# Blocks 0 to 2 of h behind four stages turned by VectorE and SBUF-to-SBUF moves instead of TensorE

## What is computed

```
h = x + 0.5 * swiglu(rmsnorm(h, ffn1_norm), ffn1_w_in, ffn1_w_out)
u = rmsnorm(h, mix_norm) @ w_in_mix
h = h + concat(y_pool, y_gla) @ w_out_mix
h = h + 0.5 * swiglu(rmsnorm(h, ffn2_norm), ffn2_w_in, ffn2_w_out)
x = rmsnorm(h, final_norm)
h = mixer_a(x, w_in_a, w_o_a);  x = layer_norm(ALPHA * x + h)
x = x + (p @ w_ple) * sigmoid(x @ w_ple_gate)
k, v = x @ w_kv_b;  h = mixer_b(x, w_in_b, w_o_b, k, v);  ...
```

## Time and profile before

| | us |
|---|---|
| median of 3 runs | 2770.53 (2770.22 to 2772.04) |
| the profiled execution's own time | 2770.9 |
| its span, first to last instruction | 2769.1 |
| PE busy | 2731.3 |
| DVE busy | 1527.7 |
| ACT busy | 1290.0 |
| POOL busy | 63.6 |

### The profile page before, as it was taken

The page is one execution under the profiler, slowest core; times in us unless marked ns, Lnnn a source line. Parts: engine busy times, 40 slices in busy tenths (PEclk is TensorE's granted clock), DMA queues, the critical chain, the costliest instruction groups (busy, mean ns, idle before and its releaser), DMA issues.

```text
span 2769.1 us, 34994 instructions
## 1 busy us (share of the span) xinstructions
PE 2731.3 (99%) x12382; PEld 2244.7 (81%) x12382; DVE 1527.7 (55%) x1831; ACT 1290.0 (47%) x1691; POOL 63.6 (2%) x72
## 2 busy tenths in 40 slices
PE   7999999999999999999999999999999999999998
PEld 6888888888888788888888888887888888777877
DVE  4555555555644455555555555658555566555566
ACT  4443444344544454443444344544544454554463
POOL 1000000000000000000000000030000000120000
PEclk9999999999999999999999999999999999999999
DMA  7766567666644455765566666654465565445653
GB/s 225 223 215 199 181 196 226 192 195 195 199 148 158 149 194 160 223 218 193 182 201 224 195 195 190 200 174 153 144 202 176 168 196 190 152 140 192 188 176 130
DMA packets 404697, 516.09 MB, mean 186 GB/s; under 512 B 45750, under 2 KB 257920, under 8 KB 403792
## 3 DMA queue, kind: packets, MB, share of 16 engines
q1 hardware_dynamic: 402560, 505.84, 58.3%
q0 software_dynamic: 1824, 8.37, 0.9%
q10 hardware_dynamic: 176, 0.07, 0.0%
HBM read 502.06 MB, written 2.10 MB: 182 GB/s over the span
## 4 chain that ended last, share of the span: by engine, by line
PE 95%; DVE 2%; ACT 1%; POOL 1%; DMA 1%; SPq 1%; issue 0%; ACTq 0%; DVEq 0%; POOLq 0%
PE bank L1284 30%; PE bank L1286 30%; PE bank L1285 30%; PE bank L1242 1%; DMA h<-in_x_dram 1%; DVE wlo L1550 1%; POOL rope_b L858 1%; PE bank L1005 0%; PE bank L806 0%; ACT whi L1353 0%; PE bank L790 0%; PE bank L1022 0%; PE bank L1031 0%; SPq L1149 0%; DVE isc L915 0%
## 5 line engine op out<-in xcount | busy, mean ns | idle before, releaser
L1550 DVE TENSOR_TENSOR wlo<-raw,whi 128x1024 fp32r<-128x1024 f32 (+2 forms) x976 | 1149.4, 1186 | 1047.8 <-ACT whi L1353 1041.5
L1353 ACT CAST whi<-raw 128x1024 fp32r<-128x1024 f32 (+2 forms) x976 | 984.2, 1016 | 1206.8 <-PE bank L1286 1201.4
L1284 PE MATMUL bank<-whi,p_hi 128*128 128x512 f32 x2016 | 797.4, 396 | 4.0 <-DVE wlo L1550 4.0
L1286 PE MATMUL bank<-whi,p_lo 128*128 128x512 f32 x2016 | 786.9, 390 | 0.0
L1285 PE MATMUL bank<-wlo,p_hi 128*128 128x512 f32 x2016 | 786.6, 390 | 0.0
L1284 PE MATMUL bank<-whi,q_hi 128*128 128x512 f32 x1696 | 665.5, 392 | 1.6 <-DVE wlo L1550 1.6
L1286 PE MATMUL bank<-whi,q_lo 128*128 128x512 f32 x1696 | 660.5, 389 | 0.0
L1285 PE MATMUL bank<-wlo,q_hi 128*128 128x512 f32 x1696 | 660.0, 389 | 0.0
L1284 PEld LDWEIGHTS bank<-whi,p_hi 128*128 128x128 f32 x2016 | 379.7, 188 | 88.9 <-issue 10.0
L1285 PEld LDWEIGHTS bank<-wlo,p_hi 128*128 128x128 f32 x2016 | 379.7, 188 | 80.2 <-issue 3.1
L1286 PEld LDWEIGHTS bank<-whi,p_lo 128*128 128x128 f32 x2016 | 379.5, 188 | 80.3
(11 more groups left out here) (265 smaller groups left out, 1032.2 us busy)
## 6 DMA issues: line engine op xcount, KB each, us to landing
raw<-in_ffn_w_in_dram SPq DMA_DIRECT2D x704, 256.0 KB, 4.4
raw<-in_ffn_w_out_dram SPq DMA_DIRECT2D x320, 256.0 KB, 3.5
raw<-in_w_in_a_dram SPq DMA_DIRECT2D x192, 256.0 KB, 3.0
raw<-in_w_in_mix_dram SPq DMA_DIRECT2D x128, 256.0 KB, 3.1
raw<-in_w_ple_gate_dram SPq DMA_DIRECT2D x128, 256.0 KB, 3.6
raw<-in_w_in_b_dram SPq DMA_DIRECT2D x128, 256.0 KB, 3.1
raw<-in_w_out_mix_dram SPq DMA_DIRECT2D x64, 256.0 KB, 3.1
raw<-in_w_o_a_dram SPq DMA_DIRECT2D x64, 256.0 KB, 3.3
```

The costliest lines, as they stand in the source:

```text
L1284: pe.matmul(o, xht, wh, start=(kt == t_first), stop=False)
L1286: ins = pe.matmul(o, xlt, wh, start=False, stop=(kt == t_last))
L1353: act.copy(whi[:, c % SPLIT, 0:n, 0:w], raw[:, c, 0:n, 0:w]).then_inc(hi_done, 1)
L1550: dve.tensor_tensor(wlo[:, c % SPLIT, 0:n, 0:w], raw[:, c, 0:n, 0:w], whi[:, c % SPLIT, 0:n, 0:w].bitcast(F32), ALU.subtract).then_inc(lo_ ...
```

## The change

`transposes` is no longer used for blocks 0 to 2 behind the four stages of `follows`; block 3 stays as it was. In its place stands the way of the hidden blocks, with pieces of its own:

- `turn_block` on DVE, directly behind `evacuate` of round k (k = 0 to 2): two 32x32-square transposes of 128x512 from h into turned.
- `move_block` on SP: 16 DMAs of 32 partitions x 1,024 bytes from turned to moved, in the load of round k+2 behind chunk 3 (for block 2 in round 0 of the next stage), waiting for the turn and for the block before to be converted.
- `block_hi` on ACT and `block_lo` on DVE in round k+1, between the splits of chunks 4 to 7 and those of the next round's chunks 0 to 3. block_hi has four instructions of 128x256; block_lo has eight of 128x128 where a gain is applied (all but gate0) and four of 128x256 in gate0.
- turned and moved lie in hidq and hidf for the first three stages, and in two new overlaid buffers for gate0.
- PE waits at round 0 of the next stage, in front of chunks 0, 2 and 4, for blocks 0, 1 and 2.

```diff
@@ planning
             if s.name in follows and nxt:
                 pair, gain = follows[s.name]
-                for k in range(s.n):
-                    where = s.before if k + 1 < s.n else nxt.before
-                    where.setdefault((k + 1) % s.n, []).extend(
-                        Batch(columns(h), pair, 4 * k + 2 * j, GAIN[gain] if gain else None) for j in range(2))
+                s.turn0, s.turn_pair, s.turn_gain, nxt.after = turned_blocks, pair, GAIN[gain] if gain else None, s
+                turned_blocks += s.n - 1
+                s.turned = (ae["turned_e"], ae["moved_e"]) if s.kind == "gate" else (turned_t, moved_t)
+                nxt.before.setdefault(0, []).extend(
+                    Batch(columns(h), pair, 4 * (s.n - 1) + 2 * j, s.turn_gain) for j in range(2))
...
+        def turned_behind(s, k, peeled, behind):
+
+            if not peeled:
+                return None
+            if s.turn0 is not None and k >= behind:
+                return s, k - behind
+            if s.after is not None and k < behind - 1:
+                return s.after, s.after.n - behind + k
             return None
@@ SP
+            def move_block(s, k):
+
+                turned, moved = s.turned
+                sp.wait_ge(blk_turned, s.turn0 + k + 1)
+                if s.turn0 + k:
+                    sp.wait_ge(blk_done, s.turn0 + k)
+                for q in range(4):
+                    for f in range(4):
+                        sp.dma_start(moved[f * QB:(f + 1) * QB, q, :, :, :], turned[q * QB:(q + 1) * QB, f, :, :, :]).then_inc(blk_moved, 16)
@@ PE
+                            if s.after is not None and c % 2 == 0 and c < 6:
+                                pe.wait_ge(blk_done, s.after.turn0 + c // 2 + 1)
@@ ACT
+            def block_hi(s, k):
+
+                act.wait_ge(blk_moved, 256 * (s.turn0 + k + 1))
+                for j in range(4):
+                    kt = 4 * k + j
...
+                    if s.turn_gain is None:
+                        ins = act.copy(dst, src)
+                    else:
+                        ins = act.activation(dst, src, ACT.Copy, scale=vec[:, s.turn_gain + kt:s.turn_gain + kt + 1])
+                ins.then_inc(blk_hi, 1)
@@ DVE
+            def turn_block(s, k):
+
+                dve.wait_ge(acc_free, s.a0 + k + 1 + FREE0)
+                for t in range(TT):
+                    ins = dve.transpose(s.turned[0][:, :, :, t, :].rearrange("p f j n -> p j f n"),
+                                        h[:, t, k * NB:(k + 1) * NB].rearrange("p (j f n) -> p j f n", j=4, f=4))
+                ins.then_inc(blk_turned, 1)
@@ DVE, round
                     if made:
                         hidden_lo(*made)
+                    block = turned_behind(s, k, peeled, 1)
+                    if block:
+                        block_lo(*block)
                     if not (peeled and k == s.n - 1):
                         first_half(s, k + 1, peeled)
...
                     evacuate(s, k, u)
+                    if s.turn0 is not None and k < s.n - 1:
+                        turn_block(s, k)
```

More of the change, by code:

```diff
@@ L98, in __init__ @@
         self.need = {}
+        self.turn0 = None
+        self.after = None
     def chunk_tiles(self, c):
@@ L206, in build @@
         nmax = small[:, 56:72].rearrange("p (b n) -> p b n", b=4)
+        turned_t, moved_t = (x[:, :, :, :, :, :].rearrange("p u f j t n -> p (u f j t n)").rearrange("p (f j t n) -> p f j t n", f=4, j=4, t=TT)
+                             for x in (hidq, hidf))
         bank = [ctx.enter_context(nc.psum_tensor(f"bank{b}", [P, NB], F32)) for b in range(8)]
@@ L261, in build @@
         follows = {"ffn1_out2": ("P", "mix"), "mix_out": ("Q", "ffn2"), "ffn2_out2": ("Q", "final"), "gate0": ("P", None)}
+        turned_blocks = 0
         for n, s in enumerate(stages):
@@ L311, in build @@
                     if k == 0 and s.kind != "ffn_out":
[L312 removed]
+                        s.need[c] = latest.get((s.pair, s.chunk_tiles(c)[-1] // 2 * 2), -1) + 1
         def batches_of(s, k, peeled):
@@ L417, in build @@
         hid_moved = [sem(f"hidden_moved_{u}") for u in range(2)]
+        blk_turned, blk_moved, blk_hi, blk_done = sem("block_turned"), sem("block_moved"), sem("block_hi_done"), sem("block_done")
         ident_in, const_in = sem("ident_in"), sem("const_in")
@@ L1180, in load @@
                                 move_hidden(*made)
+                            block = turned_behind(s, k, isinstance(k, int), 2)
+                            if block:
+                                move_block(*block)
                 paired_rounds(sp, s, load)
@@ L1330, in round_ @@
                                 pe.wait_ge(hid_done, s.hid_of.turned0 + s.chunk_tiles(c)[-1] // 2 + 1 + HID0)
-                            else:
+                            elif s.need[c]:
                                 pe.wait_ge(t_done, s.need[c])
@@ L1507, in second_half @@
                         hidden_hi(*made)
+                    block = turned_behind(s, k, peeled, 1)
+                    if block:
+                        block_hi(*block)
                 def round_(k, u):
@@ L1577, in hidden_lo, with block_lo @@
                 ins.then_inc(hid_done, 1)
+            def block_lo(s, k):
+                dve.wait_ge(blk_hi, s.turn0 + k + 1)
+                for j in range(4):
+                    kt = 4 * k + j
+                    hi_, lo_ = (pair[s.turn_pair][:, kt, :].rearrange("p (t q n) -> p t q n", t=TT, q=4)
+                                for pair in (pair_hi, pair_lo))
+                    src = s.turned[1][:, :, j, :, :].rearrange("p q t n -> p t q n")
+                    if s.turn_gain is None:
+                        ins = dve.tensor_tensor(lo_, src, hi_.bitcast(F32), ALU.subtract)
+                        continue
+                    for t in range(TT):
+                        ins = dve.scalar_tensor_tensor(lo_[:, t, :, :], src[:, t, :, :], vec[:, s.turn_gain + kt:s.turn_gain + kt + 1],
+                                                       hi_[:, t, :, :].bitcast(F32), ALU.mult, ALU.subtract)
+                ins.then_inc(blk_done, 1)
+            def turn_block(s, k):
+                dve.wait_ge(acc_free, s.a0 + k + 1 + FREE0)
+                for t in range(TT):
+                    ins = dve.transpose(s.turned[0][:, :, :, t, :].rearrange("p f j n -> p j f n"),
+                                        h[:, t, k * NB:(k + 1) * NB].rearrange("p (j f n) -> p j f n", j=4, f=4))
+                ins.then_inc(blk_turned, 1)
             def rms(n):
```

4 lines of the change are left out of this document (added).

## The result

The changed kernel takes **2818.76 us** (median of 4 runs, 2817.76 to 2821.1) against 2771.28 before (4 runs, 2770.22 to 2773.76): **1.017 times as long, 95% interval 1.0157 to 1.0184**, slower by 47.5 us. The forecast was 2812, with a range of 2790 to 2838. The profiled execution took 2821.1 us, with a span of 2819.3, 50.2 longer than the span before.

A forecast was written before the change was run, and what follows sets the result against it. PE, busy 2731.3 of 2769.1 us, was taken as the bound. Stages 2 x 15.0 - 1.4 + 7.6 plus 5.6 of clock gave +41.8 on 2770.9, 2812.7, and 2812 for the median; range 2790 to 2838.

The forecast's parts named there:

- clock behind them: Slow clock after each stage's last wait: 2.0 us for each ffn_out2, 1.6 for gate0, together +5.6.
- terms of the chain: From round end: evacuation 3.8 us, turns to 5.1, moves 16.5, hi 18.0, lo 20.4, first split ready at 21.6.
- both bounds, 0.33 and 1.18: Issue time per move on SP, kept at 0.59 us: 0.33 takes 4.2 off the chain, twice 0.59 adds 9.4.
- first and second rival: First: moves cost issue by bytes, 1.18 us each, 2925 (4%). Second: issue 0.33, chain nearly fits, 2770 (4%).
- price of an issue: SP's issue of each move: 590 ns by the trace, against the skill's dispatch of about 50 ns.
- repeating delay: Late first splits delay the next block's chain: period 22.5 us against 16.3 of PE in ffn_out2, two more waits of 6.2.
- absorption: A slower PE round inside a stage takes its loss out of the next wait, as the chain sets the pace.
- fourth rival: Clock not absorbed: all roughly nine long waits bring a slow stretch that counts, 1.6 to 2.0 each, 2823 us; 12%.
- "no wait": mix_out's first block: split ready at 21.6 us against a PE round of 21.8, so PE does not wait.
- third rival: Moves are hidden: first split ready within 16.3 us of round end, whole -10.7 stays, 2760 us; 5%.
- the whole 10.7: PE time of the removed transposes of h: 12 blocks at 0.89 us in four stages, -10.7 us.

The follow-up runs named there:

- e5: Changed kernel, but both ffn_out2 stages keep their blocks on PE; only mix_out and gate0 are changed: 2782.25 us, ratio 1.0034 against the kernel before.
- e10: The kernel before, unchanged, run and profiled again for a third trace: 2772.39 us.
- e1: Changed kernel without any of its moves, hi and lo made from turned (values wrong): 2766.09 us, ratio 0.9979 against the kernel before.
- e3: Changed kernel with hi and lo moved behind the next round's first four weight splits, all 16 moves kept: 2771.19 us, ratio 1.0003 against the kernel before.
- e4: Changed kernel with hi and lo one round later, behind chunk 4's split, and two moved buffers: 2766.37 us, ratio 0.9976 against the kernel before.
- e9: The kernel before, unchanged, run and profiled again for a second trace: 2770.57 us.

## Why the prediction was right

The mechanism, the sign and most of the size held (47.5 us measured, some 41 forecast): a chain of turn, moves, hi and lo that is longer than a round, in front of the first split. By stage, forecast and measured (differences of stage lengths between the two traces, us):

| | forecast | measured |
|---|---|---|
| ffn1_out2 | +15.0 | +15.38 |
| ffn2_out2 | +15.0 | +15.41 |
| mix_out | -1.4 | +0.62 |
| gate0 | +7.6 | +7.73 |
| clock behind them (mix_pool, a_index, b_kv) | +5.6 | 2.55 + 2.70 + 1.70 = +6.95 |
| all other stages | 0 | +4.1 |
| sum | +41.8 | +50.2 |

The misses (2.0 in mix_out, 1.4 in the clock, 4.1 in the other stages) are all upwards, so the forecast did not come out near the time by errors that cancel.

**The terms of the chain.** In block 0 above: the additions end 3.75 us into the round (3.8 forecast), the turns take 1.30 (1.3), from the turn's end to hi are 11.8 (11.4; 11.36 in block 1, from 727.77 to 739.13), hi 1.70 (1.57), lo 2.19 (2.2), and PE's next round starts 22.1 us in (21.6). The following ones last 22.4 and 22.6 (22.5). The 1,024-byte rows, for which no row of before had a price, are issued in 591 ns each, the value that was kept; both bounds, 0.33 and 1.18, are out, and with them the first and second rival. gate0's chain, DVE, SP, ACT and DVE again, from a round start at 2276.42:

```profile
2284.21 1.30 DVE L1649 STREAM_TRANSPOSE turned_e<-h 128x512 f32<-128x512 f32 x2
...
2285.54 10.03 SPq L1178 DMA_DIRECT2D moved_e<-turned_e  x16
...
2296.85 1.33 ACT L1430 CAST p_hi<-moved_e 128x256 fp32r<-128x256 f32 x4 [8.24 <-DMA moved_e<-turned_e]
...
2298.21 1.43 DVE L1638 TENSOR_TENSOR p_lo<-moved_e,p_hi 128x256 fp32r<-128x256 f32 x4 [8.19 <-ACT p_hi L1430]
```

The turn ends 9.1 in, hi starts at 20.4, lo at 21.8, and the next round at 24.5, each within 0.2 of the working. Its two periods were 25.2 and 26.0 (25.5; the prediction's own terms add to 25.4).

On the price of an issue the prediction compared two different things. The Trainium skill, "DMA: Bandwidth & Descriptors", "Anatomy of one DMA", has its 50 ns or so of sequencer dispatch for a DMA issued by GpSimd. No run here issues a move there, so that figure is neither confirmed nor refuted, and it was no price for SP's queue. The runs show 591 ns on SP's queue and 614 on ACT's.

**The repeating delay** held: three waits a stage, not one. The single waits are smaller than the forecast 6.2 wherever the round before ran in part at the lower clock, while the starts stay 22.4 and 22.6 apart. PE in the changed ffn1_out2 and behind it, three windows:

```profile
721.00:724.40 3.40, 2.42 (x6) 1.97 (x7) 3.40 (x4) 1.24 (x2) 0.00 (x0) 0.50 0.54 145
...
745.00:748.40 3.40, 3.40 (x10) 2.66 (x9) 3.40 (x5) 0.00 (x0) 0.00 (x0) 0.51 0.85 246
765.00:771.80 6.80, 4.89 (x12) 3.86 (x13) 6.37 (x9) 2.58 (x4) 0.00 (x0) 0.53 0.97 319
```

The first belongs to a stretch of 6.8 us at the 1.2 GHz level after the wait of 5.64; the next wait is 3.01 instead of 6. That is the absorption the prediction counted on. The measured median lies nearer to the fourth rival's 2823 than to 2812, but not by that rival's mechanism, which charged every stretch: the ffn_out2 stages, with stretches inside them, are within 0.4 of the forecast. The last row is the stretch behind ffn1_out2, and it is paid: mix_pool's +2.55.

**mix_out is the term that was off**, -1.4 forecast and +0.62 measured. Its first chain was to end 21.6 us into a round of 21.77, with 0.2 to spare, and ended after 22.6. The part that grew is the moves:

```profile
1022.66 11.13 SPq L1178 DMA_DIRECT2D hidf<-hidq  x16
...
1035.08 1.71 ACT L1432 ACTIVATE q_hi<-hidf,vec 128x256 fp32r<-128x256 f32 x4 [5.36 <-DMA hidf<-hidq]
```

12.4 from the turn's end to hi instead of 11.4. The median issue was 591 ns, the longest 1701. Of the 12 groups of 16 moves, five had one issue of 1.05 to 1.70 us and took 10.5 to 11.1 us; the other seven took 10.0 to 10.2. mix_out had two of the five. In a chain nothing gives such an issue back, so a sum of medians is short for it, by up to 1 us a block here. e5, with the same mix_out, ends it at -0.24. The margin of 0.2 us on which "no wait" rested was smaller than that.

**The clock** cost 6.95 behind the stages against 5.6, since two of its three stretches lasted 6.8 us, where that of the earlier trace rows had 3.4.

**All other stages** were forecast at nothing and gave +4.1: mix_qk 1.61, a_gate 1.65, the start 0.6, the rest small. mix_qk's is the stretch that e10 shows in the kernel before. a_gate's stands behind a wait of 2.46 us that both kernels have (at 2073.72 in the kernel before); PE there in the changed kernel, and its window:

```profile
2112.74 1.45 PE L1274 MATMUL bank<-con,tm 128*128 128x128 f32 x8 [2.46 <-DVE p_lo L1611]
```

```profile
2114.00:2117.40 3.40, 3.40 (x10) 2.68 (x10) 1.38 (x2) 0.60 (x2) 0.00 (x0) 0.55 0.27 101
```

It came in the profiles of all nine kernels with changed ffn_out2 stages, and in none of the three of before, nor in e5's. Why it follows them stays open. In the median of the runs these add less: 47.5 against 50.2.

**The third rival, faster at 2760, could not have come true**, in this order of the queues, and the prediction put its price wrongly. It took the whole 10.7 for granted once the moves are hidden. e1 has no moves and reaches 2766.1: the queues alone keep 1.85 us in each ffn_out2. e1 takes over 11 us of moves out of the chain and its first split is still ready only 16.7 us in, so no price of the moves reaches the 16.3 at which that rival was to decide. What hides the moves is not a shorter chain but a later reader: e3, with the same 16 moves, is level with before, and e4 is below it. The Trainium skill, "VectorE: DVE Perf Modes", "Rules for kernel authors", advises TensorE for a 128x128 transpose that may go to PSUM. This change agrees with it by 47.5 us; e4, whose reader stands a round later, speaks against it by 0.24%.

## What to carry to other kernels

Cost a new producer by the time from its input to its first reader on each in-order queue, not by engine shares: here 10.7 us left a 99% busy engine and 58 came back, though DVE and ACT, which took work over, were free for 45 and 53% of the time. If the chain is longer than a round, give its reader another round and buffer before shortening the chain, and then count what its DMA issues add to the queue that also feeds the weights. A margin of a few tenths of a microsecond behind 16 issues in a row is none.

## What the hardware showed beyond that

- The issue of an SBUF-to-SBUF move has the same price at both sizes tried: a median of 591 ns at 16 KB with 512-byte rows and at 32 KB with 1,024-byte rows, and 614 ns on ACT's queue. The issues of the weight loads have medians of 328 to 432 ns in the changed kernel.
- Five of 192 of the changed kernel's issues took 1.05 to 1.70 us, and their groups of 16 took 10.5 to 11.1 us instead of 10.0 to 10.2.
- A PE with no idle time in front can still be granted half its clock for 3.4 us, in some runs of a program and not in others (e9 and e10 at 835.00), here behind 3.6 us of matmuls with 16 or 1 rows. In the changed kernel each of the eight waits of 2.6 to 5.6 us for a weight split went with a stretch of 3.4 or 6.8 us at half the clock.
